# Two transformer blocks on one core: order of weight and modulation loads in the first projection, later modulation sums, and early q rows

## What is computed

```python
# first block
h = rms_norm(x, norm_mix_g);  z = h @ w_in
u_a, v_a = gelu(z[..., :512]), gelu(z[..., 512:1024])          # "gelu", 8 tiles
q_b, k_b, v_b = ...                                            # "qk" 8 tiles, "vb" 4 tiles
f_logit = z[..., 2560:2568] + f_bias                           # "forget", 8 columns
out_a = spatial_gating(u_a, v_a, sg_ln_g, sg_w, sg_b)
out_b = forgetting_attention(q_b, k_b, v_b, f_logit)
x = x + concat([out_a, out_b]) @ w_out;   x = x + conv_ffn(...)
# second block, for two layers i
shift, scale, gate = split(silu(c) @ w_mod[i] + b_mod[i], 3)   # "modulation"; the same with c_ctx
hx = modulate(rms_norm(x, norm_g[i]), shift_x, scale_x)        # then attention, w_o, residual
```

## Time and profile before

| | us |
|---|---|
| median of three runs | 3204.71 |
| lowest, highest | 3197.19, 3213.44 |
| the profiled execution | 3206.6 |
| span of the core in it | 3204.9 |
| PE busy in the span | 2941.1 (92%) |
| DVE, POOL, ACT busy | 1725.0, 1067.0, 981.7 |

### The profile page before, as it was taken

How to read it: one execution, slowest core, us unless ns; L and a number is a source line. 1 busy time by engine, 2 the same in 40 slices (tenths; PEclk the granted TensorE clock), 3 DMA queues, 4 the chain that set the end, 5 groups by cost and what they waited for, 6 DMA issues and landing times. The chain is left out here.

```text
span 3204.9 us, 44121 instructions
## 1 busy us (share of the span) xinstructions
PE 2941.1 (92%) x16440; PEld 2420.2 (76%) x16440; DVE 1725.0 (54%) x2485; ACT 981.7 (31%) x1727; POOL 1067.0 (33%) x657
## 2 busy tenths in 40 slices
PE   3789899999999999989999998889889698999998
PEld 2578787878888888777877877878778477877776
DVE  4654254475455554555557337878743553067754
ACT  1112165231111111131101217767640200167731
POOL 1433312464554445432213221223233432311222
PEclk6899999999999999999999998999999899999999
DMA  2354460121111111113345312211111032342111
GB/s 86 125 166 159 125 135 26 40 73 39 46 46 59 46 39 46 39 56 115 115 147 181 119 58 104 80 71 50 58 35 39 26 125 92 110 124 51 28 40 66
DMA packets 214038, 255.18 MB, mean 80 GB/s; under 512 B 9385, under 2 KB 182766, under 8 KB 213886
## 3 DMA queue, kind: packets, MB, share of 16 engines
q1 hardware_dynamic: 198306, 189.68, 19.9%
q10 hardware_dynamic: 15584, 63.51, 5.0%
HBM read 187.56 MB, written 65.60 MB: 79 GB/s over the span
## 5 line engine op out<-in xcount | busy, mean ns | idle before, releaser
L977 PE MATMUL ps<-hh,w_parts 128*128 128x512 f32 (+2 forms) x2560 | 1000.4, 391 | 74.4 <-POOL hl L797 34.6
L978 PE MATMUL ps<-hl,w_parts 128*128 128x512 f32 (+2 forms) x2560 | 983.2, 384 | 0.0
L979 PE MATMUL ps<-hh,w_parts 128*128 128x512 f32 (+2 forms) x2560 | 981.0, 383 | 0.0
L977 PEld LDWEIGHTS ps<-hh,w_parts 128*128 128x128 f32 x2560 | 488.1, 191 | 191.5 <-issue 62.8
L758 POOL TENSOR_TENSOR w_parts<-w_raw,zero 128x1024 fp32r<-128x1024 f32 x140 | 289.6, 2069 | 972.2 <-PE ps L979 818.1
L978 PEld LDWEIGHTS ps<-hl,w_parts 128*128 128x128 f32 x2560 | 490.5, 192 | 104.4 <-issue 5.7
L979 PEld LDWEIGHTS ps<-hh,w_parts 128*128 128x128 f32 x2560 | 488.7, 191 | 99.8
L760 POOL TENSOR_TENSOR w_parts<-w_raw,w_parts 128x1024 fp32r<-128x1024 f32 x140 | 340.9, 2435 | 11.0
L1882 ACT ACTIVATE f_y<-f_z,convv 128x1024 f32<-128x1024 f32 x44 | 54.8, 1244 | 511.5 <-DVE f_z L2447 511.3
L2637 DVE TENSOR_SCALAR_CACHE_REDUCE b_s<-ps 128x640 f32<-128x640 f32 (+1 forms) x128 | 100.0, 781 | 96.0 <-PE ps L1523 96.0
L2447 DVE TENSOR_TENSOR f_z<-ps,f_rs 128x1024 f32<-128x1024 f32 x44 | 53.9, 1224 | 181.4 <-PE ps L979 181.2
(11 more groups left out here) (338 smaller groups left out, 4870.4 us busy)
## 6 DMA issues: line engine op xcount, KB each, us to landing
w_mod_sb<-in_w_mod SPq DMA_DIRECT2D x16, 1536.0 KB, 7.1
w_raw<-in_w_up SPq DMA_DIRECT2D x44, 512.0 KB, 3.7
w_raw<-in_a_w_in SPq DMA_DIRECT2D x32, 512.0 KB, 4.1
d_raw<-in_w_down SPq DMA_DIRECT2D x22, 512.0 KB, 4.5
w_raw<-in_w_in SPq DMA_DIRECT2D x20, 512.0 KB, 4.9
za_parts<-z_hi ACTq DMA_DIRECT2D x16, 640.0 KB, 3.0
za_parts<-z_lo ACTq DMA_DIRECT2D x16, 640.0 KB, 4.1
d_even<-za_parts SPq DMA_DIRECT2D x16, 640.0 KB, 6.6
```

Of the source, the lines that this page charges most:

```text
L977: pe.matmul(out_, w_hi, x_hi, start=start, stop=False)
L978: pe.matmul(out_, w_hi, x_lo, start=False, stop=False)
L979: return pe.matmul(out_, w_lo, x_hi, start=False, stop=stop)
```

## The change

SP's order in "gelu" is written out: the raw tiles of pairs 0 and 1 before the wait for the norm, then in turn the modulation tiles of pair i and, ahead of them, the raw tiles of pair i + 1. PE's sums of a modulation tile (i,s) stand behind tile (i+1,s), those of the last pair behind the first q tile. The last v tile counts its row blocks (`project_leaving`, semaphore `h_left`), and SP loads the four q transfers into `hh` and `hl` of head pair 0 when row block 4 has been read. DVE scales an "a_v" tile before it runs that tile's burst.

```diff
@@ weight_tiles
-            def tile_pair(i):
+            def raw_pair(i):
                 for s in range(2):
                     sp.wait_ge(w_split[s], i + W0[name][s] + 1)
...
+
+            def tile_pair(i):
+                raw_pair(i)
                 if parts_stored is not None and isinstance(i, int):
                     for s in range(2):
                         sp.wait_ge(stored[s], 16 * parts_stored[s] + 16)
                 if mod_layer is not None:
                     for s in range(2):
-                        if norm:
-                            sp.wait_ge(n_low[s], 4 * (SPLITS[norm] + 1) + 1)
+                        mod_tiles(i, s)
+
+            if norm:
+                for i in range(2):
+                    raw_pair(i)
+                for s in range(2):
+                    sp.wait_ge(n_low[s], 4 * (SPLITS[norm] + 1) + 1)
+                for s in range(2):
+                    mod_tiles(0, s)
+                with sp.Fori(1, tiles // 2 - 1) as i:
+                    raw_pair(i + 1)
                     for s in range(2):
                         mod_tiles(i, s)
-
+                for s in range(2):
+                    mod_tiles(tiles // 2 - 1, s)
+                return
             tile_pair(0)
@@ block.sync
-            def fa_load_q(j):
+            def fa_load_q2(j):
                 sp.dma_start(a_q2[j % 2][0:DH].bitcast(F32), z1_parts[0, j * P:(j + 1) * P, :].rearrange("(a p) n -> p a n", p=DH)).then_inc(
                     fa_loaded[j % 2], 16)
+
+            def fa_load_q1(j):
                 for a, to in enumerate((hh, hl)):
                     for part in range(2):
                         sp.dma_start(to[part * DH:(part + 1) * DH, 4 + j, X_COLS].bitcast(F32),
...
             fa_load_v(0)
+            sp.wait_ge(h_left, 4 + 1)
+            fa_load_q1(0)
             for s in range(2):
                 sp.wait_ge(w_used[s], W0["w_out"][s] + 1)
-            fa_load_q(0)
+            fa_load_q2(0)
             for s in range(2):
                 sp.wait_ge(stored[s], 16 * (Z0["vb"][s] + 2) + 16)
-            fa_load_q(1)
+            fa_load_q2(1)
+            fa_load_q1(1)
...
                 sp.wait_ge(fa.scored, 2 * QB * (j - 1))
-                fa_load_q(j)
+                fa_load_q2(j)
+                fa_load_q1(j)
@@ project
             if norm:
                 project_first(pe, name, segs, norm)
-                if mod_layer is not None:
-                    mod_sums(pe, mod_layer, 0, 0)
             with pe.Fori(1 if norm or begun else 0, tiles // 2) as i:
                 for s in range(2):
                     project_tile(pe, name, i, s, segs)
                     if mod_layer is not None:
-                        mod_sums(pe, mod_layer, i + (s - 1), 1 - s)
+                        mod_sums(pe, mod_layer, i - 1, s)
@@ block.tensor
             project_tile(pe, "forget", 0, 0, LATENT_SEGS)
-            mod_sums(pe, 0, 3, 1)
...
-            for s in range(2):
-                pe.wait_ge(mod_kept[s], 4 + 1)
             for j in range(4):
                 project_tile(pe, "qk", j, 0, LATENT_SEGS)
+                if j == 0:
+                    for s in range(2):
+                        mod_sums(pe, 0, 3, s)
+                    for s in range(2):
+                        pe.wait_ge(mod_kept[s], 4 + 1)
                 spatial_turn(j)
                 project_tile(pe, "qk", j, 1, LATENT_SEGS)
                 spatial_mix(j)
-            project(pe, "vb", 4, LATENT_SEGS)
+            project_leaving(pe, "vb", 4, LATENT_SEGS)
@@ block.scalar
-                act.wait_ge(h_left, k + 1)
+                act.wait_ge(h_left, KT - 1 + k + 1)
@@ scale_turned
             for n in range(8):
-                for k in range(KT):
-                    for v in range(2):
-                        modulate_step(dve, 1, n // 2, n % 2, k, v)
...
                 scale_tile(dve, name, n // 2, n % 2, divmod(n - 1, 2) if n else None)
+                for k in range(KT):
+                    for v in range(2):
+                        modulate_step(dve, 1, n // 2, n % 2, k, v)
```

## The result

The changed kernel takes 3189.96 us (median of 17 runs, 3182.46 to 3197.3) against 3206.52 for the kernel before (17 runs): a ratio of 0.9945, 95% interval 0.9936 to 0.9954, so 17.6 us. The forecast was 3205, no change. The profiled run has a span of 3189.2 us.

The account below looks back on a forecast made before the run. TensorE does nearly all the work, so only its waits near edited lines were priced: 10.6 us lost in the first projection, 5.5 and 4.5 gained later, together +0.6 on 3204.71, forecast 3205 us, range 3182 to 3213.

Parts of the forecast that it names:

- part 1: First projection, reordered loads and later sums: `spatial_turn` starts at 258.6 against 247.97 us, 10.6 us lost.
- Held as at 121.83 and 159.16: First projection: VectorE's bursts hold GpSimd's split of tile (1,1) until 133.5, so TensorE waits 7.5 us.
- Held through both bursts: Forget weights: GpSimd's split is held through VectorE's last two bursts, free at 215.4; TensorE waits 17.8 us.
- rival B: First projection: only the forget split gets in; total gain 12.7 to 16 us, 3191 us; chance 0.22.
- case D: First projection: the split of (1,1) and the forget split both get in, 23.5 us gained, 3181 us; chance 0.16.
- the q split: Behind the forget tile: the weight split of the first q tile needs 4.8 us, as before the change.
- Part 2: Last v tile: four q loads go out early, TensorE starts sooner; 5.5 us gained.
- Part 3: Second layer's v tiles: scaling is done while the modulation burst waits for its weights; 4.5 us gained.
- E: Forget and first q tile: the clock stays at 1.2 GHz, 18.5 us slower, 3224 us; chance 0.07.
- F: Last v tile: the remaining q load lands as late as before, 5.5 us lost, 3210 us; chance 0.05.
- C: First projection: only the split of (1,1) gets in, tile starts 9.1 us earlier, 3196 us; chance 0.14.
- case A: Whole kernel, with both first-projection splits held: no change, 3205 us, own range 3197 to 3213; chance 0.36.

Follow-up runs that it names:

- Held by force: Changed kernel plus two GpSimd waits holding the split of tile (1,1) and the forget split until VectorE's bursts are done; ratio 1.0009 to the kernel before.
- alone, 5.6: Kernel before with only the four early q loads within the last v tile; ratio 0.9964, -11.6 us.
- part 3 alone: Kernel before with only the scaling moved ahead of the modulation burst in the second layer's v tiles; ratio 0.9986, -4.5 us.
- the kernel of half steps: Kernel before with every VectorE modulation step made two of 192 columns, plus GpSimd probes in second-layer bursts; one run, 3228.24 us.
- the kernel that beats both: Changed kernel with the last modulation pair's sums put back ahead of the first q tile; 3174.93 us, ratio 0.9899 to the kernel before.
- the kernel with the stand between the bursts: Kernel before with an empty six-turn loop on VectorE between the two bursts of each modulation pair; ratio 0.9980.

## Why the prediction was wrong, point by point

**The failed step** is in part 1 of the sum: "Held as at 121.83 and 159.16", which put a wait of 7.5 us ahead of (1,1), and "Held through both bursts", which put 17.8 us ahead of forget. Neither split was held. PE did not wait for the one (0.54 us for the sums is all) and waited 2.92 us for the other. The choice stands in rival B: "its 0.8 us behind the start of the burst is nearest to 121.83 (0.75 behind) and 159.16 (0.32), while 175.59 came 1.8 behind." The distance was measured to the wrong mark. Behind VectorE's last stand the three lie 8.8, 8.4 and 1.8 us, 18, 16 and 4 steps; the new arrivals lie one and two steps behind it (0.45 and 0.74 us). By the right mark they are nearest to 175.59, the one that got in. The profile had it: the row at 113.01 has idle time in brackets, the one at 121.08 has none. It also had a second split let in, at 184.37, where the prediction counted one: the 15.00 us of that burst are the price of two splits, some 3.8 us each, as in the changed kernel (11.26). The Trainium skill, page SBUF — State Buffer, section "Who interferes with whom", has the hold last one instruction. That gives what these two arrivals did (case D), but neither the 9.15 us of the earlier trace rows nor the 10.22 at 124.25, so the measurement decides, and no single length of the hold fits both.

**Part 1.** Taken +10.6; 10.9 gained at 260 us, so 21.5 us off. Held by force the same kernel stands 11.7 behind. Right in it: the loads (sums at 124.71, predicted 124.6), the wait for forget if let in (2.92, predicted 2.8), the q split (4.83 and 4.8), `s_v` (6.96 and 6.4). Against case D the gain is 2.6 us short; 1.5 of it is tile (1,1), which ran at a clock of 0.87 (first row; behind it tile (2,0), at the whole clock):

```profile
126.20:138.90 12.70, 12.70 (x50) 0.87 0.81 283
140.40:151.60 11.20, 11.17 (x49) 1.00 0.33 107
```

(stretch, length, PE busy, granted clock, DMA share, GB/s).

**Part 2.** Taken 5.5, measured 5.7 and, alone, 5.6; a wait of 5.25 us is left, the 5.1 of landing. SP issued the early loads from 373.98 and the last at 378.22, 4.2 us apart as worked out (384.9 and 389.14).

**Part 3.** Taken 4.5: 6.3 in the changed kernel, 3.8 alone. The turn waits 0.31 us for ScalarE instead of 6.98, as said. Next late is the split, as said: PE waits 2.67 us, since POOL came at 1664.07, thirteen steps into a run, and was held to its end (3.17). With part 3 alone the burst waits 7.74 us for its weights instead of 5.96 and ends later against the turn; the sums wait 1.95 us as well.

**Rivals.** E did not come: the clock over forget and the first q tile was 0.79 and 0.87, not 0.65. F did not come. B and C were halves of what came, D nearly all of it; the measured gain of 17.6 us lies between B's 13 to 16 and D's 23.5. That the time fell inside the stated range is owed to these rivals, which had 0.52 of the chances together, and not to case A's mechanism.

**What went back.** The changed kernel lost 6.8 of its 23.1 us between 1700 us and the end, against the one profile of before. Some 5 of it, 2.4 at 1805 to 1850 us and 2.6 at 2800 to 2900, is no work of the change: in the first stretch every other trace loses against that profile too (2.2 to 3.1 us in all thirteen), in the second all but two (1.2 to 2.6), whatever was edited, so the profile of before was quick there. In the first stretch its granted clock stayed whole, where the other thirteen have 0.93 or 0.96. In the second it is a wait for ScalarE at the start of the second attention: 4.24 us in that profile, 6.69 in the changed kernel's, 4.06 and 4.25 in the two that lose nothing. The rest, some 2 us, was not traced.

## What to carry over

Before costing a wait between two engines that exclude each other, look for the time since the other engine last stood still, not for the place in its loop; a loop boundary is no stand. If a hold of many microseconds lies on the path, put a wait or an arrival where the other engine stands anyway, or make it stand. An arrival at the edge of such a rule made traces of the same code differ by 5 to 6 us here, as much as part 2 or part 3 is worth, so read a term near it from several traces.

## What the runs showed of the hardware that was not expected

- POOL with two inputs is let in by a run of VectorE's modulation steps (384 columns, 0.53 us each) only while at most six or seven steps have been done since VectorE's last stand; from eight on it waits for the run's end, up to 15.35 us in the kernel of half steps. With half steps (0.33 us) it is held at eight steps, 2.4 us behind the restart.
- An instruction that is let in early is hardly hindered (2.04 for 1.89 us), but VectorE stands for both POOL instructions of the split: 11.26 us for the 14 steps of 7.49, and 15.00 with two splits let in.
- A loop of two turns on VectorE cost nothing beside a step of 0.61 us; six turns made a stand of 0.63 us.
- TensorE's granted clock was 0.87 over the tile behind the changed kernel's wait of 0.54 us and 1.00 over the same tile of the kernel that beats both, behind 0.39 us.
- Two traces with nearly the same wait of PE for a weight split differ in the clock behind it: 2.04 us in the kernel before, granted clock 1.00 from 1805 to 1850 us; 2.06 us in the kernel with the stand between the bursts, 0.93 over the same work.
